# Expert layers of a hybrid decoder step: the eight sample rows as a unit in front of the last prompt unit, instead of a tail behind it

## The reference: what is computed

```
s = einsum('thpd,hpnd->thpn', q, sub_keys);  sv, si = top_k(s, 16)
cand = sv[..0..] + sv[..1..];                top_s, top_i = top_k(cand, 16)
idx  = the 8*16 expert numbers of a row;     gate = softmax(top_s)
h    = einsum('td,ted->te', x, u_tab[idx])
out  = einsum('te,ted->td', gelu(h) * gate, v_tab[idx])
```

## Time and profile before

| | us |
|---|---|
| median of 3 runs | 4147.41 (4142.09 to 4147.81) |
| the profiled execution: its own time | 4148.73 |
| its span (first to last instruction) | 4147.0 |
| PE busy in the span | 3517.3 (85%) |
| DVE busy | 2579.0 (62%) |
| ACT busy | 1476.8 (36%) |
| POOL busy | 1350.2 (33%) |
| DMA | 1208.32 MB, mean 291 GB/s |
| mean granted clock of TensorE, share of full speed | 0.918 |

### The profile page before, as it was taken

The page is one execution under the profiler, slowest core; times in us unless marked ns, Lnnn a source line. Parts: engine busy times, 40 slices in busy tenths (PEclk is TensorE's granted clock), DMA queues, the critical chain, the costliest instruction groups (busy, mean ns, idle before and its releaser), DMA issues. The chain is left out here.

```text
span 4147.0 us, 47996 instructions
## 1 busy us (share of the span) xinstructions
PE 3517.3 (85%) x13207; PEld 1887.4 (46%) x13207; DVE 2579.0 (62%) x6388; ACT 1476.8 (36%) x4177; POOL 1350.2 (33%) x1196
## 2 busy tenths in 40 slices
PE   7997888888888797888878789898888897888887
PEld 6877784433333343333333467544333343333332
DVE  3665443677677777777734434337777777676774
ACT  2451211344343434444412332224344444443442
POOL 0014320344434444444400011015444344444442
PEclk9997889999999998999879889999999999999998
DMA  2220002899999999999931025439999999999997
GB/s 93 71 79 13 12 12 110 329 416 401 413 401 403 410 403 409 407 403 416 410 130 59 11 116 208 159 112 417 419 408 408 407 412 404 412 405 403 410 420 325
DMA packets 195538, 1208.32 MB, mean 291 GB/s; under 512 B 28744, under 2 KB 40272, under 8 KB 58720
## 3 DMA queue, kind: packets, MB, share of 16 engines
q0 software_dynamic: 153600, 1133.58, 67.0%
q1 hardware_dynamic: 41696, 72.24, 5.1%
HBM read 1197.88 MB, written 7.86 MB: 291 GB/s over the span
## 5 line engine op out<-in xcount | busy, mean ns | idle before, releaser
L1274 PE MATMUL po<-ring,diag 128*128 128x512 f32 x4096 | 1998.0, 635 | 406.0 <-ACT diag L1065 403.1
L1011 POOL DMA_INDIRECT ring<-in_uv,idx x1024 | 1167.3, 1140 | 1756.4 <-PE po L1274 1354.5
L1140 DVE SCALAR_TENSOR_TENSOR ring<-ring,xn 128x1024 f32<-128x1024 f32 x1024 | 1226.2, 1223 | 587.3 <-DMA ring<-in_uv,idx 531.5
L1274 PEld LDWEIGHTS po<-ring,diag 128*128 128x128 f32 x4096 | 780.8, 200 | 1446.8 <-issue 767.8
L1059 ACT ACTIVATE hg<-hs 128x1 f32<-128x1 f32 x1024 | 203.5, 199 | 1352.3 <-DVE ring L1140 1346.8
L1065 ACT ACTIVATE diag<-const,hgg 128x128 f32<-128x128 f32 x1024 | 411.4, 402 | 66.0 <-issue 4.6
L1061 ACT ACTIVATE hgg<-hg,gate 128x1 f32<-128x1 f32 x1024 | 302.0, 295 | 37.0
L1195 PE MATMUL wide<-xnT,w 128*128 128x512 f32 (+1 forms) x512 | 266.4, 606 | 2.1 <-ACT q L1029 1.5
L292 PE MATMUL acc<-xnT,w 128*128 128x260 f32 x1024 | 230.2, 386 | 0.7 <-ACT inp L413 0.7
L292 PEld LDWEIGHTS acc<-xnT,w 128*128 128x128 f32 x1024 | 196.1, 192 | 38.0 <-issue 7.2
L1196 PEld LDWEIGHTS wide<-xnT,w 128*128 128x128 f32 x512 | 99.5, 194 | 118.6 <-issue 111.9
(11 more groups left out here) (466 smaller groups left out, 3956.5 us busy)
## 6 DMA issues: line engine op xcount, KB each, us to landing
w<-in_w_gdn SPq DMA_DIRECT2D x32, 512.0 KB, 3.5
w<-in_w_peer SPq DMA_DIRECT2D x32, 512.0 KB, 7.9
ring<-in_uv,idx POOLq DMA_INDIRECT x1024
out_ssm_s<-states SPq DMA_DIRECT2D x4, 1024.0 KB
ring<-in_w_gdn_out SPq DMA_DIRECT2D x4, 1024.0 KB, 10.5
ring<-in_w_mla_out SPq DMA_DIRECT2D x4, 1024.0 KB, 10.9
wq<-in_w_uq SPq DMA_DIRECT2D x1, 3072.0 KB, 14.1
x<-in_x_prompt SPq DMA_DIRECT2D x1, 2048.0 KB
```

What stands on the lines that cost most here:

```text
L1011: pool.indirect_dma_start(out=ring[:, c % RING, :], out_offset=None, in_=uv, in_offset=bass.IndirectOffsetOnAxis(ap=idx[t % 2][:, c:c + 1] ...
L1140: dve.scalar_tensor_tensor(ring[:, c % RING, 0:D], ring[:, c % RING, 0:D], 1.0, xn[:, t, :], ALU.mult, ALU.mult, accum_out=hs[a][:, c:c + ...
L1274: last = pe.matmul(po[a][:, HALF * e:HALF * e + HALF], diag[:, c % RING, :], ring[:, c % RING, D + HALF * e:D + HALF * e + HALF], start=c ...
```

## The change

The tail behind the last unit is gone. In front of the last unit (last head, t = 3) now stands a **sample unit**, one position for each of the eight sample rows, and what follows a row's dot is done for that row alone:

- POOL: the eight sample gathers come before the last unit's sixteen. Those of the last unit's steps 0 to 7 wait for `spv`, which PE counts when a sample row's position is through.
- PE: for b = 0 to 7 it spreads row b (`sample_row`), then takes `values(b)`, four matrix multiplications (eight records) into `pT`. `values(b - 1)` stands in front of `sample_row(b)`. The odd rows use `po[1]` instead of `po[0]`.
- ACT: Gelu of one row (128x1) and its scaling by the gate, written to the diagonal of `sac`; the diagonal was made by two DVE operations and a constant `same`, which is no longer loaded.
- DVE: the eight sample dots come before the last unit's dots; the copies out of `pT` and the addition to the residual (3 us of work in the tail) stand behind the last unit's step 3. The last prompt block is added at the very end.
- Turning the indices and the gates moves to t = 2 (PE at steps 2 and 12, DVE behind the dots of steps 5 and 14). In the last head, the exponentials of the sample gates move from step 8 to step 1 of t = 2, and the gates from step 13 to step 9.

```diff
+        vals = pT[:, :, :].rearrange("p s n -> p (s n)")
 
         def row_of(b):
 
-            return (wide if b % 2 == 0 else po[0])[:, :]
+            return (wide if b % 2 == 0 else po[1])[:, :]
...
+                            pool.wait_ge(s["turned_i"], 1)
+                            for j in range(NS):
+                                pool.wait_ge(s["pv"], u * TOPK - RING + j + 1)
+                                pool.indirect_dma_start(out=ring[:, j, :], out_offset=None, in_=uv,
+                                                        in_offset=bass.IndirectOffsetOnAxis(ap=sidxT[:, j:j + 1], axis=0)).then_inc(s[f"landed{j}"], 16)
                         apart(pool, at("top", u, TOP_STEPS))
                         for c in range(TOPK):
                             if first and t == 0 and c == RING // 2:
                                 pool.wait_ge(s["o_made"], 2 * T)
-                            if c >= RING or t or not first:
+                            if last and t == NT - 1 and c < RING:
+                                pool.wait_ge(s["spv"], c + 1)
+                            elif c >= RING or t or not first:
                                 apart(pool, at("pv", u, c - RING + 1))
                             pool.indirect_dma_start(out=ring[:, c % RING, :], out_offset=None, in_=uv,
                                                     in_offset=bass.IndirectOffsetOnAxis(ap=idx[t % 2][:, c:c + 1], axis=0)).then_inc(s[f"landed{c % RING}"], 16)
...
-                pool.wait_ge(s["flipped"], 2)
-                for j in range(NS):
-                    pool.wait_ge(s["pv"], UNITS * TOPK - RING + j + 1)
-                    pool.indirect_dma_start(out=ring[:, j, :], out_offset=None, in_=uv,
-                                            in_offset=bass.IndirectOffsetOnAxis(ap=sidxT[:, j:j + 1], axis=0)).then_inc(s[f"landed{j}"], 16)
...
+                        if last and t == NT - 1:
+                            for b in range(NS):
+                                act.wait_ge(s["sdot"], b + 1)
+                                act.activation(shs[:, 1, b:b + 1], shs[:, 0, b:b + 1], ACT.Gelu).then_inc(s["sgelu"], 1)
+                                act.wait_ge(s["sgelu"], b + 1)
+                                act.wait_ge(s["turned_g"], 1)
+                                act.wait_ge(s["szero"], 1)
+                                act.activation(sac[:, b, b:b + 1], shs[:, 1, b:b + 1], ACT.Copy, scale=sgateT[:, b:b + 1]).then_inc(s["sact"], 1)
...
-                            if c == WEIGH_C and t == 2:
+                            if (t, c) == ((2, 1) if last else (2, WEIGH_C)):
...
+                        if not more:
+                            for b in range(NS):
+                                dve.wait_ge(s["rowed"], b + 1)
+                                after(dve, at(f"landed{b}", u, 16))
+                                dve.scalar_tensor_tensor(ring[:, b, 0:D], ring[:, b, 0:D], 1.0, row_of(b), ALU.mult, ALU.mult,
+                                                         accum_out=shs[:, 0, b:b + 1]).then_inc(s["sdot"], 1)
                         for c in range(TOPK):
-                            after(dve, at(f"landed{c % RING}", u, 16 * (c // RING + 1)))
+                            after(dve, at(f"landed{c % RING}", u, 16 * (c // RING + 1 + (not more))))
                             dve.scalar_tensor_tensor(ring[:, c % RING, 0:D], ring[:, c % RING, 0:D], 1.0, xn[:, t, :],
                                                      ALU.mult, ALU.mult, accum_out=hs[a][:, c:c + 1]).then_inc(s["dot"], 1)
+                            if last and t == 2 and c == 5:
+                                dve.wait_ge(s["flip_i"], 1)
+                                dve.tensor_copy(sidxT[:, :], pT[:, 0, 0:NS]).then_inc(s["turned_i"], 1)
+                                dve.memset(sac[:, :, :], 0.0).then_inc(s["szero"], 1)
+                            if last and t == 2 and c == 14:
+                                dve.wait_ge(s["flip_g"], 1)
+                                dve.tensor_copy(sgateT[:, :], pT[:, 1, 0:NS]).then_inc(s["turned_g"], 1)
                             if c == 3 and not more:
-                                dve.wait_ge(s["flip"], 1)
-                                dve.tensor_copy(sidxT[:, :], pT[:, 0, 0:NS]).then_inc(s["flipped"], 1)
-                                dve.tensor_copy(sgateT[:, :], pT[:, 1, 0:NS]).then_inc(s["flipped"], 1)
-                                dve.memset(sac[:, :, :], 0.0).then_inc(s["szero"], 1)
+                                dve.wait_ge(s["spv"], NS)
+                                for j in range(4):
+                                    dve.tensor_copy(svals[:, QUARTER * j:QUARTER * j + QUARTER], vals[32 * j:32 * j + NS, :]).then_inc(s["smoved"], 1)
+                                dve.wait_ge(s["smoved"], 4)
+                                dve.tensor_tensor(core.xs[:, :], svals[:, :], core.xs[:, :], ALU.add).then_inc(s["sadded"], 1)
...
-                            if c == 13 and t == 2:
+                            if (t, c) == ((2, 9) if last else (2, 13)):
...
+                def values(b):
+                    pe.wait_ge(s["sact"], b + 1)
+                    for j in range(4):
+                        last = pe.matmul(vals[32 * j:32 * j + 32, :], sac[:, b, :], ring[:, b, D + QUARTER * j:D + QUARTER * j + QUARTER], start=b == 0, stop=b == NS - 1)
+                    last.then_inc(s["spv"], 1)
...
-                            pe.wait_ge(s["sgate"], 2 * H)
-                            pe.transpose(pT[:, 0, 0:NS], sidx[:, :], core.const[:NS, C_ID, 0:NS])
-                            pe.transpose(pT[:, 1, 0:NS], sgate[:, :], core.const[:NS, C_ID, 0:NS]).then_inc(s["flip"], 1)
+                            for b in range(NS):
+                                if b >= 1:
+                                    if b == 1:
+                                        pe.wait_ge(s["turned_g"], 1)
+                                    values(b - 1)
+                                if b >= 2:
+                                    pe.wait_ge(s["sdot"], b - 1)
+                                sample_row(b)
+                            values(NS - 1)
                         for c in range(TOPK):
                             after(pe, at("diag", u, c + 1))
                             for e in range(2):
                                 last = pe.matmul(po[a][:, HALF * e:HALF * e + HALF], diag[:, c % RING, :], ring[:, c % RING, D + HALF * e:D + HALF * e + HALF],
                                                  start=c == 0, stop=c == TOPK - 1)
                             last.then_inc(s["pv"], 1)
-                            if last_head and t == NT - 1 and c == 12:
-                                pe.wait_ge(s["added"], UNITS - 1)
-                                pe.wait_ge(s["q_out"], 4 * H)
-                                for b in range(2):
-                                    sample_row(b)
+                            if last_head and t == 2 and c == 2:
+                                pe.wait_ge(s["stop"], TOP_STEPS * H)
+                                pe.transpose(pT[:, 0, 0:NS], sidx[:, :], core.const[:NS, C_ID, 0:NS]).then_inc(s["flip_i"], 1)
+                            if last_head and t == 2 and c == 12:
+                                pe.wait_ge(s["sgate"], 2 * H)
+                                pe.wait_ge(s["turned_i"], 1)
+                                pe.transpose(pT[:, 1, 0:NS], sgate[:, :], core.const[:NS, C_ID, 0:NS]).then_inc(s["flip_g"], 1)
...
-                for b in range(2, NS):
-                    pe.wait_ge(s["sdot"], b - 1)
-                    sample_row(b)
-                pe.wait_ge(s["sact"], 2)
-                pe.wait_ge(s["added"], UNITS)
-                for b in range(NS):
-                    for j in range(4):
-                        last = pe.matmul(po[1][32 * j:32 * j + 32, 0:QUARTER], sac[:, b, :], ring[:, b, D + QUARTER * j:D + QUARTER * j + QUARTER], start=b == 0, stop=b == NS - 1)
-                last.then_inc(s["spv"], 1)
```

More of the change, by code:

```diff
@@ L923, in peer @@
     with Marks(core, "peer", o_w0=16, o_w1=16, gain=16, o_made=2, o_added=2, square=1, mean=1, root=1, inverse=1, row=1, turned=2, copied=1, copied2=1,
-               inp=48, w0=16, w1=16, q_first=2, first_out=2, q_made=2, q_out=4, scored=1, top=TOP_STEPS, exped=1, gate=2,
-               dot=TOPK, gelu=TOPK, factor=TOPK, diag=TOPK, pv=TOPK, added=1, sscored=1, stop=TOP_STEPS, sexped=1, sgate=2, flip=1,
-               flipped=2, rowed=1, sdot=1, sgelu=1, szero=1, sact=2, spv=1, smoved=2, sadded=1,
+               inp=32, w0=16, w1=16, q_first=2, first_out=2, q_made=2, q_out=4, scored=1, top=TOP_STEPS, exped=1, gate=2,
+               dot=TOPK, gelu=TOPK, factor=TOPK, diag=TOPK, pv=TOPK, added=1, sscored=1, stop=TOP_STEPS, sexped=1, sgate=2, flip_i=1, flip_g=1,
+               turned_i=1, turned_g=1, rowed=1, sdot=1, sgelu=1, szero=1, sact=1, spv=1, smoved=4, sadded=1,
```

(28 more changed lines are left out.)

2 lines of the change are left out of this document (1 added, 1 removed).

## The result

The changed kernel took **4183.68 us** (median of 4 runs, 4180.03 to 4185.21), the kernel before 4145.82 (4 runs, 4142.09 to 4147.81): a ratio of 1.0091 [1.0079, 1.0103], 0.9% slower. The forecast was 4176, the range 4157 to 4186.

A forecast was written before the change was run, and what follows sets the result against it. Gathers were taken to bound the kernel, compute at half clock its tail. Layer terms of +15.3 and +13.4 us, +28.7, raised the profiled 4148.73 to 4177.4; the median, 1.3 lower, became 4176, range 4157 to 4186.

The forecast's parts named there:

- What bounds the kernel: In the peer phases gathers bound, 2.48 us each; in the tail, compute by itself at half TensorE clock.
- A position at half clock: Sample unit: row to dot 3.66, dot to PE 1.87, values 0.85, together 6.4 us per sample row.
- Which clock: TensorE in the sample unit: full clock for 4.2 us, then half, as 8-deep rows had lost it before.
- Start of the unit: Sample unit's start on PE: some 0.2 us later through the moves into t = 2, at 2043.9 and 4067.5.
- Behind the unit: Last unit: step 8's dot 12.0 us after the sample unit, seven gathers 17.4, then 5.5 to the end.
- V: End of the sample unit, its start plus 49.1 us: 2093.0 in layer 0 and 4116.6 in layer 1.
- Sum: Both layers: +15.3 and +13.4 us, together +28.7, giving a median of 4176 us.
- What costs nothing: ACT table loads, DVE's wait at step 14, sample result behind step 3, load of `same`: covered; 4 us if covers fail.
- half and half: Rival, sample unit: clock returns for part, position 5.4 us, end 5.9 us sooner per layer, 4164 us; chance 0.10.
- Full clock: Rival, sample unit: full clock throughout, position 4.4 us, together -2 us, 4145 us; chance 0.08.
- the point from which the sign decides: Sample unit: the position length separating slower from faster, about 4.4 us.
- DMA-paced: Rival: landed gathers hide the sample unit's slowness, -10.5 and -10.4 us, 4126.5 us; chance 0.04.

The follow-up runs named there:

- no spread rows: Changed kernel without the spread rows, sample dots multiplying with the prompt block's xn, so the sample result is wrong: 4129.34 us, ratio 0.996.
- rows early: Changed kernel with the eight rows spread beforehand, behind step 7 of t = 0, 1 and 2, and copied to SBUF: 4139.05 us, again 4135.71.
- gaps filled: Changed kernel with four extra 128-deep multiplications, result unused, on PE in front of each values(b): 4156.6 us, ratio 1.0023.
- rows ahead: Changed kernel with rows 0 and 1 spread first and row b + 2 behind values(b) on PE: 4151.17 us, ratio 1.0008.
- changed again: Changed kernel unaltered, run once more beside the kernel before: 4180.5 us, ratio 1.0075.
- `same` kept: Changed kernel with the load of the constant `same` and its buffer put back, though nothing reads it: 4184.66 us, ratio 1.0085.
- the kernel before and its variant: The variant is the kernel before, tail included, plus only the moves into t = 2 of the last head: 4147.78 us, ratio 1.001.
- mixed: Changed kernel with sample positions alternating with steps 0 to 7 of the last prompt unit: 4134.93 us, ratio 0.9973; again 4137.64, 0.9977.

## Why the prediction was right, point by point

- **What bounds the kernel**: right. Paced by gathers, the stretch is about 102 us long (no spread rows, rows early). The changed kernel's 127 to 130 are a unit that lets the ring run empty; the 111 to 114 of before are the tail.
- **A position at half clock**: the chain was as forecast, and 6.67 us instead of 6.4. Row to dot took 3.81 (2057.68 to 2061.49), not 3.66, because the row itself lasts 3.77 on PE where it lasted 3.62 in the earlier trace rows. Dot to values was 1.85 (1.87 forecast). Values to row took 1.02, not 0.85. The tail's 64 records of the earlier trace rows had run partly at full clock, but only in their last 0.6 us, which accounts for some 0.05; a group of eight by itself costs more than an eighth of 64 in a row (at full clock too: 0.57 to the next row in gaps filled, where the forecast had 0.5). Seven spacings of 0.3 us are most of the unit's excess: 51.7 us (2039.37 to 2091.10) for 49.1 (its own terms add up to 49.3). This is the mis-sized term of the unit, +2.6 per layer. Why a row behind values is 0.15 longer was not tried.
- **Which clock**: right. It fell 3.7 and 4.0 us behind the unit's first row (4.2 taken), and stayed at 0.50 for 54.6 and 51.2 us, to beyond the unit's end. (The fall of the earlier trace rows comes out at 4102.2, 3.2 us behind its rows, where the forecast had 4102.4 and 3.3.) In rows ahead PE was busy 19.74 of 20 us at 0.52. The Trainium skill's rule ("TensorE: Matmul & The Clock Gate", why this matters for your kernels), which names long idle gaps as what costs the clock, doesn't cover that. The changed kernel alone couldn't show it, for PE had idled 2 us just before the fall.
- **Start of the unit**: forecast +0.2 us against before. From the first dot of t = 2 to the unit's start on PE it is 42.5 us in layer 0 (44.7 before) and 41.4 in layer 1 (41.4 before). The other two profiles with the changed kernel's code there (changed again, `same` kept) have 42.3 and 43.0 in layer 0, 42.5 and 42.5 in layer 1, and the second of before has 44.8 and 41.4. So the start comes about 2 us sooner in layer 0 and up to 1 later in layer 1. The forecast had only the transposes and one exponential in it. Which of the moves gives the 2 us isn't shown.
- **Behind the unit**: V + 34.9 forecast; 35.7 and 33.9 measured. Inside, two errors cancel. Step 8's gather was issued at V + 4.55 (2095.65) and its data had landed by 5.8 us later, so its dot came at V + 10.3 and not V + 12.0; then the next seven dots took 19.8 us in layer 0 and not 17.4 (18.0 in layer 1). In layer 0 dots 9 and 10 came 3.5 and 4.0 us behind the ones before; the gather of the first had been issued 2.94 us behind step 8's, the second I can't account for. The 8.0 us from issue to dot were too many. The 5.8 here are an upper bound, since the dot didn't wait, and lie below both of the earlier trace rows; the next dot did wait, and stood 6.3 us behind its gather's issue (2098.59 to 2104.93; 6.3 in layer 1 too). By the Trainium skill ("DMA: Bandwidth & Descriptors", anatomy of one DMA) the transfer takes 4.4, an estimate. So the trace is between my figure and the page's.
- **Sum**: forecast +15.3 and +13.4 in the stretch; measured +16.3 and +14.9, 31.1 for 28.7, in the two profiles that were compared. That it came so near is in part luck, for the errors in its terms have both signs. By the balance: start -2.5 and -0.1, unit +2.6 and +2.6, behind it +0.8 and -1.0.
- **The medians** say +37.9 [32.7, 42.7] in the first set of runs and +33.9 [25, 36.5] in the second, the stretch +32.3 and +30.6 against the mean of before. The difference, if it is one, lies outside the changed code. From the end of layer 0's phase to the next stretch it is 1913.3, 1915.6 and 1916.8 us in the kernel before and its variant, and 1918.9, 1922.1 and 1921.9 in the changed one and its variant, 1918.5, 1921.8 and 1920.6 in rows ahead, gaps filled and no spread rows, while rows early and mixed lie between 1916.9 and 1921.1 in two profiles each. So all ten profiles of the changed kernel and its variants lie above all three of the kernel before and its variant, by 0.1 to 9 us. That hints at something systematic of a few us, but executions scatter by more (4136 to 4156 for one unchanged kernel), and what makes it stays open.
- **What costs nothing**: DVE's wait for the gates at step 14 lasted 2.03 us in layer 0 (2.00 in layer 1) and delayed nobody, for PE worked on without a gap meanwhile; the copies behind step 3 stood among prompt dots whose data had landed. The load of `same` is covered by the run that kept it.
- **The rivals**: two of the three were made real by an experiment, which is the best support for the step that chose among them; half and half wasn't. Full clock gave a position of 4.43 (4.4 worked out) and, in layer 0, a stretch of 113.7 us, equal to before's 112.0 to 113.6, so the point from which the sign decides was about right. DMA-paced gave -20.7 in the stretch (-20.9 worked out).
- **What would show it**: sample dots 6.67 apart for 6.4; clock 0.50 for 55 and 51 us for 45; step 8's dot 10.3 us behind the last values for 12; 5.5 us from the last dot to the end, as forecast; the DMA share 0.61 over the 45 us at half clock and 0.50 in its second half, where I had written 0.4: I had left out that the sample gathers were still queued for the unit's first 12 us.

## What to carry to other kernels

When a unit is put into a pipeline that a queue of transfers paces, work out its period as the sum of its dependent steps, at the lower clock too. If it is longer than the transfer's period, the ring can empty, and then most of the excess is lost: here eight positions were 33.5 us longer than eight gathers (6.67 for 2.48), and the stretch was 27.7 and 25.3 us longer than without spread rows. Starting the next step's input ahead of the current step's output cut the period from 6.67 to 4.72 us at the same clock; alternating the slow unit with one that does keep pace hid most of it (207.0 and 208.8 us of stretch, for 203.9 paced by DMA). A replaced tail should be compared with what it cost beyond its transfers, here only some 10 us a layer.

## What the runs showed of the hardware that I had not expected

Useless work can pay: 2 us of 128-deep multiplications in each position kept the granted clock at 1.00 for 20 us, where it had been 0.50, and shortened the position by 2.2 us. It isn't dependable: in layer 1 of the same execution the clock averaged 0.86 over 20 us, with the same instructions. And in mixed, where a prompt step gives each pair as much 128-deep work (1.98 us in 4.43), it averaged 0.74. And a clock of 0.66 on average did no harm in the kernel without spread rows, since PE was not what the dots waited for.
